# Attention's row maxima taken per 512-query chunk and strewn over two heads, in a hybrid decoder block on one Trainium2 core

## The chip, the core and the metric

The kernel runs on one core of one Trainium2 chip. Its engines are TensorE (PE, matrix products into the accumulation banks, PSUM), VectorE (DVE), ScalarE (ACT), GpSimd (POOL) and SyncE (SP), which here only issues DMAs. Each engine runs its own instructions in order; they wait for one another through semaphores. The metric is the device time of one execution in microseconds (us).

## The reference, cut to what matters

```python
q = (rmsnorm(c_q, g_cq) @ w_uq).reshape(B, S, MLA_HEADS, 96)      # 8 heads, S = 2048
...
for i in range(S // Q_BLOCK):                                     # 128 queries at a time
    s = (jnp.einsum("bqhd,bkhd->bhqk", q_nope[:, q0:q1], k_nope[:, :q1])
         + jnp.einsum("bqhr,bkr->bhqk", q_rope[:, q0:q1], k_rope[:, :q1])) * scale
    p = jax.nn.softmax(jnp.where(causal, s, -jnp.inf), axis=-1)
    outs.append(jnp.einsum("bhqk,bkhd->bqhd", p, v[:, :q1]))
```

This is causal attention over 2048 positions with 8 heads of 96 query and key dimensions and 64 value dimensions. Ahead of it stands one input projection, behind it a gated mixer, a cross-attention into 256 memory tokens and a mixture of 64 experts. All of it is float32, which the kernel makes of fp32r products: each operand x is split into a rounded high part xh and a low part xl = x - xh, and a product is the sum of three.

## The kernel before, in words

The program is a row of blocks: `front` (projections, in 512-token chunks), `attention`, `mix`, cross-attention, routing, experts, combine. Engines meet at a barrier between blocks. The change is in `attention`, with a little in the tail of `front`.

**Units.** Scores are made transposed (keys on partitions, 512 queries in the columns), so that the exponentials can be used as operands at once. A head has 40 units `cols[u] = (c, j)`: query chunk c (0 to 3) against key tile j (0 to 4c+3). The last four units of each chunk lie on the diagonal and have 512, 384, 256 and 128 columns. For unit u PE makes `scores` (three products, L791, L792, L794, and a bf16 mask product L796 on the diagonal) into the ring of four banks `psS`; ACT takes two exponentials of it (`pf` L909, `ph` L910, the second rounded); DVE (odd u, L983) or POOL (even u, L1027) subtracts them to `pl`; PE makes three `products` with the values (L810 to L812). In its loop PE stands at unit u, makes the scores of unit u+3 and the products of unit u-2, so the scores of a head's units 0 to 2 are made at units 37 to 39 of the head before.

**Maxima.** Softmax needs each row's maximum before its first exponential. It is subtracted inside the score product: rows 96 and 97 of `qh` hold minus the maximum (its high and low part) and those of `kh` hold ones. To find it, PE makes plain high-part scores with queries on partitions, in 40 steps `(i, c)` (query tile i, key chunk c, L828, with a mask L830 on the diagonal) into two banks `psA`, and DVE reduces each to `nm` (L944). A last, 41st step turns the 2048 minima: DVE folds `nm` to `mm` (L947), PE transposes it (L821), DVE splits it to `mh` and `ml` (L951, L953), SP sends both to rows 96 and 97 (L716, L717), and the first score product of the head waits for that (`m_in`). The steps of head h+1 are made inside units 11 to 34 of head h, some 1.7 a unit (`a_at`). Head 0's stand by themselves ahead of the units, and the first sixteen alternate with `memory_values`, products for the later cross-attention; before them stand four `memory_keys` (L835).

**Row splits.** A head's q, k and v come by five DMAs (`load`, L707 to L711) to `qraw`, `kraw`, `vraw`. ACT makes the high parts in nine pieces (512 columns of q four times, of k four times, then v; L886, L882) at units 2 to 10, POOL the low parts at units 4, 7, ..., 28 (L1012, L1014); for head 0 DVE makes half of them (L971). SP loads head h+2 once head h+1's splits are done.

Of the kernel before, what the change touches and what calls it, by code (L numbers as in the profile page):

```python
# [16 lines left out]
P = 128  # L17
# [4 lines left out]
CH = 512  # L22
# [77 lines left out]
def front(nc, cst, vec, x, g_mix, w_slabs, pos, w_uq, w_uk, w_uv, gates_d, conv_d, qn_d, qr_d, kn_d, kr_d, v_d,  # L100
          mem, g_mem, w_kv, hh0, hl0, wk_mem, wv_mem, memT, kv_in):
# [9 lines left out]
    with ExitStack() as ctx:  # L111
# [35 lines left out]
        acc = [s_.ps(f"acc{i}", [P, CH]) for i in range(2)]  # L147
# [114 lines left out]
        def _(pe):  # L262
# [71 lines left out]
            for q in range(NC_):  # L334
                for n in range(N):
# [12 lines left out]
                    slab(q, n)  # L348

# [291 lines left out]
def attention(nc, cst, masks, qn_d, qr_d, kn_d, kr_d, v_d, o_d, l_d, wk_mem, wv_mem, memT, kmT, vm, kv_in, km_d, vm_d,  # L641
              w_a, w_b, wb_raw, wa_raw, ar, lr, aT, mixer):
# [7 lines left out]
    rows = [(i, c) for i in range(NT) for c in range(i // 4 + 1)]  # L650
    cols = [(c, j) for c in range(NC_) for j in range(4 * c + 4)]
    NU, NA = len(cols), len(rows) + 1
    RING, AHEAD, PIECES = 4, 3, 2 * NC_ + 1
    PR, LAG = 8, 2
    LO_AT = {4 + 3 * n: n for n in range(PIECES)}
    OUT_AT = {8: 0, 16: 1, 28: 2}
    A0, A1 = 11, 35
    a_at = {}
    for v in range(NA):
        a_at.setdefault(A0 + v * (A1 - A0) // NA, []).append(v)  # L660
    KA, VA = QKD + 2, VD + 2
    with ExitStack() as ctx:
# [16 lines left out]
        mh = s_.sb("mh", [NT, P], F32R)  # L679
        ml = s_.sb("ml", [NT, P], F32R)  # L680
# [3 lines left out]
        psS = [s_.ps(f"psS{i}", [P, CH]) for i in range(RING)]  # L684
# [20 lines left out]
        def _(sp):  # L705
# [30 lines left out]
            load(1)  # L736
            sp.wait_ge(kv_act, 2)
# [30 lines left out]
            for e in range(2):  # L768
                sp.dma_start(lr[e * VD:(e + 1) * VD, :, :], l_d[e:H:2, 0:CM].unsqueeze(0).broadcast_to([VD, H // 2, CM])).then_inc(mixer["ar_in"], 16)
            for c in range(1, NC_):  # L770
                store(H - 1, c)
# [5 lines left out]
        def _(pe):  # L777
            def scores(h, s, u, wait_max):
# [35 lines left out]
            def maxima(h, s, v):  # L814

                b = (s * NA + v) % 2

                pe.wait_ge(a_max, NA * h + v + 1)
                if v == NA - 1:
                    pe.wait_ge(mmin, h + 1)  # L820
                    nc.tensor.transpose(psA[b][0:NT, 0:P], mm_[:], ident).then_inc(a_mm, 1)  # L821
                    return
                i, c = rows[v]
                if v == 0:
                    pe.wait_ge(split_a, PIECES * h + PIECES)
# [19 lines left out]
            for h in range(XH):  # L845
                memory_keys(h)
            pe.wait_ge(set_, 9)
            for v in range(NA):
                maxima(0, 0, v)
                if v < 2 * KD:  # L850
                    memory_values(v // KD, v % KD)
            pe.wait_ge(kv_act, 2)
            pe.wait_ge(kv_dve, 4)
            for u in range(AHEAD):
                scores(0, 0, u, u == 0)

            def head(h, s, more, prev):
                for u in range(NU):
                    if u + AHEAD < NU:
                        scores(h, s, u + AHEAD, False)  # L860
                    elif more:
                        scores(h + 1, 1 - s, u + AHEAD - NU, u + AHEAD == NU)
                    if more:
                        for v in a_at.get(u, []):
# [11 lines left out]
        def _(act):  # L876
            def split(h, s, n):
# [6 lines left out]
                t = slice(n % NC_ * CH, (n % NC_ + 1) * CH)  # L884
                d, r = ((qh, qraw), (kh, kraw))[n // NC_]
# [6 lines left out]
            for b in range(2):  # L892
                act.wait_ge(kv_mm, XH + b + 1)
# [8 lines left out]
            def head(h, s, more, prev):  # L902
                for u in range(NU):
# [11 lines left out]
                    if more and 2 <= u < 2 + PIECES:  # L915
                        if u == 2:

                            act.wait_ge(pv, NU * h + PR)
                        split(h + 1, 1 - s, u - 2)
# [8 lines left out]
        def _(dve):  # L928
# [9 lines left out]
            def top(h, s, v):  # L938
                b = (s * NA + v) % 2
                if v < NA - 1:  # L940
                    i, c = rows[v]
                    w = min(CH, (i + 1) * P - c * CH)
                    dve.wait_ge(a_mm, NA * h + v + 1)
                    V.tensor_reduce(nm[:, i, c:c + 1], psA[b][:, 0:w], AX, ALU.max, negate=True).then_inc(a_max, 1)  # L944
                    return
                dve.wait_ge(a_max, NA * h + v + 2)
                V.tensor_reduce(mm_[:].unsqueeze(2), nm[:], AX, ALU.min).then_inc(mmin, 1)  # L947
                dve.wait_ge(a_mm, NA * h + v + 1)

                dve.wait_ge(m_in, 32 * h + 16)  # L950
                V.tensor_copy(mh[:], psA[b][0:NT, 0:P]).then_inc(mhd, 1)  # L951
                dve.wait_ge(mhd, h + 1)
# [1891 lines left out]
```

## Time and profile before

| | |
|---|---|
| median of 3 runs | 2920.02 us (2916.92 to 2920.36) |
| profiled execution, its time and its span | 2914.94 us, 2913.1 us |
| busy in the span: PE, DVE, ACT, POOL | 92%, 57%, 48%, 23% |
| attention block | 856 to 1423 us of the span |
| mean granted TensorE clock | 0.964 of full speed |

PE's busy time counts pipelined matmuls with modelled ends, so 92% does not say that PE runs at its peak. In the attention block PE is near full in most stretches; what matters is where it isn't, and what ended those waits.

### The profile page before, as it was taken

Reading aid. Unit: us, or ns where it says so; the run is one execution under the profiler, and the core shown is the slowest. Engines: PE = TensorE matmul, PEld = TensorE weight load, DVE = VectorE, ACT = ScalarE, POOL = GpSimd, SP = SyncE. Lnnn points to the kernel's source line nnn. Section 1 sums busy time; section 2 is a strip of 40 time slices with the busy share of each in tenths; the row PEclk is TensorE's granted clock in tenths of the full one; section 3 lists DMA queues with packets and bytes.
Section 4 is the critical chain, followed back from the end, with each engine's and each line's share of the span. In section 5 each row is a group of like instructions: output and inputs, shape, how many; then the busy total and the mean of one; then the engine's idle time right before and its main releaser. Section 6 shows DMA issues by size and latency. Waiting matters only on the chain. (4 is left out here: it accounts for less than half of the span.)

```text
span 2913.1 us, 37842 instructions
## 1 busy us (share of the span) xinstructions
PE 2670.8 (92%) x12830; PEld 2083.5 (72%) x12830; DVE 1669.3 (57%) x2262; ACT 1387.2 (48%) x2316; POOL 665.4 (23%) x708
## 2 busy tenths in 40 slices
PE   6999999999998999999799999899967999999980
PEld 5777787787775666666689898677656777777760
DVE  3623624524426666655554453465566888888858
ACT  4334334324323666667611112543416777777853
POOL 0000000000003555555322220000003444444420
PEclk9999999999998999999899999999978999999995
DMA  4253353354442112212345344232267999999978
GB/s 167 83 189 130 109 171 115 124 171 169 131 134 48 37 39 55 47 37 75 108 131 150 112 134 160 84 109 102 77 255 267 370 373 374 374 383 387 374 279 353
DMA packets 168851, 508.67 MB, mean 175 GB/s; under 512 B 40448, under 2 KB 69760, under 8 KB 140576
## 3 DMA queue, kind: packets, MB, share of 16 engines
q1 hardware_dynamic: 150016, 472.56, 47.4%
q0 software_dynamic: 18720, 34.64, 3.2%
q8 instruction: 64, 1.05, 0.1%
q14 instruction: 51, 0.42, 0.0%
HBM read 432.21 MB, written 108.33 MB: 186 GB/s over the span
## 5 line engine op out<-in xcount | busy, mean ns | idle before, releaser
L487 DVE TENSOR_TENSOR fr_wl<-fr_raw,fr_wh 128x1024 fp32r<-128x1024 f32 x128 | 156.8, 1225 | 470.5 <-ACT fr_wh L358 470.2
L358 ACT CAST fr_wh<-fr_raw 128x1024 fp32r<-128x1024 f32 x128 | 134.0, 1047 | 493.0 <-PE fr_acc L282 493.0
L2547 DVE TENSOR_TENSOR ex_gl<-ba_raw,ex_gh 128x2048 fp32r<-128x2048 f32 x128 | 293.2, 2292 | 101.8 <-ACT ex_gh L2460 101.8
L2460 ACT CAST ex_gh<-ba_raw 128x2048 fp32r<-128x2048 f32 x128 | 245.2, 1917 | 39.5 <-PEq L2055 39.5
L909 ACT ACTIVATE at_pf<-at_psS 128x512 f32<-128x512 f32 (+1 forms) x320 | 178.3, 558 | 167.1 <-PE at_psS L794 84.2
L1027 POOL TENSOR_TENSOR at_pl<-at_pf,at_ph 128x512 fp32r<-128x512 f32 (+1 forms) x160 | 195.4, 1221 | 258.7 <-ACT at_ph L910 258.2
L983 DVE TENSOR_TENSOR at_pl<-at_pf,at_ph 128x512 fp32r<-128x512 f32 (+2 forms) x160 | 145.7, 914 | 139.7 <-ACT at_ph L910 136.5
L944 DVE TENSOR_REDUCE at_nm<-at_psA 128x1 f32<-128x512 f32 (+2 forms) x320 | 183.0, 605 | 63.2 <-PE at_psA L828 43.1
L2397 PE MATMUL ex_psG<-ex_gh,ex_xh 128*128 128x512 f32 x512 | 200.7, 392 | 6.7 <-DVE ex_xl L2552 5.3
L2398 PE MATMUL ex_psG<-ex_gl,ex_xh 128*128 128x512 f32 x512 | 200.3, 391 | 0.0
L2399 PE MATMUL ex_psG<-ex_gh,ex_xl 128*128 128x512 f32 x512 | 200.1, 391 | 0.0
L1003 POOL CAST at_vh<-all_cst 128x32 fp32r<-128x32 f32 x2 | 0.5, 226 | 855.6 <-POOLq L111 855.6
L910 ACT ACTIVATE at_ph<-at_psS 128x512 fp32r<-128x512 f32 (+1 forms) x320 | 177.4, 554 | 0.0
L1239 PE MATMUL mx_psO<-mx_wo_hi,mx_mT 128*128 128x512 f32 x512 | 158.1, 390 | 2.1 <-DVE ea_wo_lo L1372 2.1
L1283 ACT CAST mx_mT<-mx_m 128x256 fp32r<-128x256 f32 x64 | 26.0, 406 | 240.1 <-DVE mx_m L1424 240.1
L282 PE MATMUL fr_acc<-fr_hh,fr_wh 128*128 128x512 f32 x512 | 137.2, 411 | 2.9 <-DVE fr_wl L487 2.9
L282 PE MATMUL fr_acc<-ea_hh,fr_wh 128*128 128x512 f32 x512 | 137.8, 412 | 2.0 <-DVE ea_hl L505 2.0
L828 PE MATMUL at_psA<-at_kh,at_qh 96*128 96x512 f32 (+2 forms) x320 | 118.6, 427 | 19.6 <-DVE at_nm L944 17.6
L791 PE MATMUL at_psS<-at_qh,at_kh 98*128 98x512 f32 (+1 forms) x320 | 122.6, 383 | 9.8 <-DMA at_qh<-at_ml 7.8
L282 PE MATMUL fr_acc<-ea_hh,fr_wl 128*128 128x512 f32 x512 | 126.9, 390 | 0.0
L282 PE MATMUL fr_acc<-fr_hh,fr_wl 128*128 128x512 f32 x512 | 126.8, 390 | 0.0
L282 PE MATMUL fr_acc<-ea_hl,fr_wh 128*128 128x512 f32 x512 | 126.6, 389 | 0.0
(367 smaller groups left out, 6469.7 us busy)
## 6 DMA issues: line engine op xcount, KB each, us to landing
ba_raw<-in_w_exp SPq DMA_DIRECT2D x192, 1024.0 KB, 19.0
fr_raw<-in_w_slabs SPq DMA_DIRECT2D x128, 512.0 KB, 3.8
gates_d<-fr_gst SPq DMA_DIRECT2D x64, 256.0 KB, 4.3
mx_gt<-gates_d SPq DMA_DIRECT2D x64, 256.0 KB, 5.3
cb_ys<-y_d SPq DMA_DIRECT2D x16, 1024.0 KB, 10.9
mx_xr<-in_x SPq DMA_DIRECT2D x8, 1024.0 KB, 7.1
x_d<-mx_xo SPq DMA_DIRECT2D x8, 1024.0 KB, 5.0
xa_xe<-x_d SPq DMA_DIRECT2D x16, 512.0 KB, 5.5
```

The lines of the kernel that those rows point to most:

```text
L282: mm = nc.tensor.matmul(acc[i % 2][:], w[:, i % 2, k, :], h[q % 2][:, k, :], start=(j == 0 and k == 0), stop=(j == 2 and k == KD - 1))
L487: V.tensor_tensor(wl[:, i % 2], raw[:, i % 2], wh[:, i % 2], ALU.subtract).then_inc(w_lo, 1)
L909: nc.scalar.activation(pf[:, u % PR, off:CH], psS[u % RING][:, off:CH], ACT.Exp)
L910: nc.scalar.activation(ph[:, u % PR, off:CH], psS[u % RING][:, off:CH], ACT.Exp).then_inc(hi, 1)
L944: V.tensor_reduce(nm[:, i, c:c + 1], psA[b][:, 0:w], AX, ALU.max, negate=True).then_inc(a_max, 1)
L1027: G_.tensor_tensor(pl[:, r, off:CH], pf[:, r, off:CH], ph[:, r, off:CH], ALU.subtract).then_inc(lo[0], 1)
L1239: mm = nc.tensor.matmul(psO[n][:], mT[:, x_, k, q * P:(q + 1) * P], wop[y_][:, k, hf * CH:(hf + 1) * CH], start=(k == 0 and i == 0), stop= ...
L2397: nc.tensor.matmul(psG[s][:], xh[:, s, f, :], gh[:, s, i, k, :], start=(f == 0), stop=False)
L2398: nc.tensor.matmul(psG[s][:], xh[:, s, f, :], gl[:, s, i, k, :], start=False, stop=False)
L2399: mm = nc.tensor.matmul(psG[s][:], xl[:, s, f, :], gh[:, s, i, k, :], start=False, stop=(f == KD - 1))
L2460: nc.scalar.copy(gh[:, s, i], raw[:, r, i, :].rearrange("p (k n) -> p k n", k=KD // 2)).then_inc(w_hi, 1)
L2547: V.tensor_tensor(gl[:, s, i], raw[:, r, i, :].rearrange("p (k n) -> p k n", k=KD // 2), gh[:, s, i], ALU.subtract).then_inc(w_lo, 1)
```

## The change: what it does

1. The maxima become a stream of 44 `steps`: 40 as before, and a turn for each 512-query chunk, two steps behind the chunk's last maximum. A turn handles four query tiles: `mh` and `ml` are now 4x128, and SP sends a chunk's 512 maxima at a time. The scores of a chunk wait for their own chunk's maxima only.
2. The stream of head h+1 is spread evenly: steps 0 to 26 over units 16 to 39 of head h (`early`), steps 27 to 43 over units 0 to 15 of head h+1 itself (`late`).
3. Head 0 has only its first 16 steps (`PRE`, chunks 0 and 1 with their turns) ahead of the units; the other 28 lie in its own units 0 to 16, and head 1's 27 early steps in its units 17 to 39.
4. ACT's row splits stand at units 3, 5, ..., 19 in the order q0, k0, q1, k1, ...; a maximum waits only for the pieces it reads. In head 0 DVE makes the low parts of k (`key_low`) between its maxima.
5. `memory_keys` of head 0 is made by PE in the tail of `front`, into a bank `bank0` that `front`, `attention` and `mix` now share; three remain in `attention`.
6. SP issues the chunks' maxima between its stores and loads, in the order given below.

The diff, cut to its core (the rest hands `bank0` through):

```diff
+            pe.wait_ge(evac, N * NC_ - 1)
+            for k in range(KD):
+                nc.tensor.matmul(bank0[:, 0:MEM], wk_mem[:, k, 0:XD], memT[:, k, :], start=(k == 0), stop=(k == KD - 1))
...
-    A0, A1 = 11, 35
-    a_at = {}
-    for v in range(NA):
-        a_at.setdefault(A0 + v * (A1 - A0) // NA, []).append(v)
+    steps = []
+    for c in range(NC_):
+        part = [(i, k) for i in range(4 * c, 4 * c + 4) for k in range(c + 1)]
+        steps += part if c == 0 else part[0:2] + [("turn", c - 1)] + part[2:]
+    steps.append(("turn", NC_ - 1))
...
+    PRE, EARLY, TURN2 = 2 * KD, 16, steps.index(("turn", 2))
...
+    BEFORE = sum(EARLY + v * NU // NE < NU for v in range(NE))
+    early, late = spread(range(BEFORE), EARLY, NU), spread(range(BEFORE, NE), 0, EARLY)
+    first_early = spread(range(BEFORE), 17, NU)
+    first_late = {**spread(range(PRE, TURN2 + 1), 0, 7), **spread(range(TURN2 + 1, NE), 7, 17)}
...
             after_split(0)
             load(1)
+            maxima(0, 0, 0)
+            maxima(0, 0, 1)
...
-            maxima(0, 0)
-
-            def head(h, s, more, more2, prev):
+
+            def head(h, s, more2, prev):
+                maxima(h, s, 2)
                 if prev:
                     store(h - 1, 3)
-                for c in range(3):
-                    store(h, c)
+                store(h, 0)
+                maxima(h, s, 3)
+                store(h, 1)
+                maxima(h + 1, 1 - s, 0)
+                store(h, 2)
                 if more2:
                     after_split(h + 1)
                     load(h + 2)
-                if more:
-                    maxima(h + 1, 1 - s)
+                maxima(h + 1, 1 - s, 1)
...
-                if wait_max:
-
-                    pe.wait_ge(m_in, 32 * h + 48)
+                if j == 0:
+
+                    pe.wait_ge(m_in, 32 * NC_ * h + 32 * c + 48)
...
-            for h in range(XH):
+            for h in range(1, XH):
                 memory_keys(h)
             pe.wait_ge(set_, 9)
-            for v in range(NA):
+            for v in range(PRE):
                 maxima(0, 0, v)
-                if v < 2 * KD:
-                    memory_values(v // KD, v % KD)
+                memory_values(v // KD, v % KD)
...
+                    for v in (late if prev else first_late).get(u, []):
+                        maxima(h, s, v)
                     if more:
-                        for v in a_at.get(u, []):
+                        for v in (early if prev else first_early).get(u, []):
                             maxima(h + 1, 1 - s, v)
...
-                    if more and 2 <= u < 2 + PIECES:
-                        if u == 2:
+                    if more and u in HI_AT:
+                        if HI_AT[u] == 0:
...
+            for v in range(PRE):
+                top(0, v)
+                if v % 3 == 0 and v > 0 and v // 3 <= NC_:
+                    key_low(v // 3 - 1)
```

**PE, where head 0's units begin.** Before, the last rows ahead of the first score product (L791) are 25 maxima that stand alone and the turn (L821):

```order
L828 MATMUL at_psA<-at_kh,at_qh 128x512 [waits at_a_max] x4
L830 MATMUL at_psA<-at_neg,at_idb 128x128
L821 MATMUL at_psA<-all_cst,at_mm 16x128 [waits at_mmin,at_a_max]
L791 MATMUL at_psS<-at_qh,at_kh 128x512 [waits at_split_p,at_m_in,at_hi,at_kv_dve,at_kv_act]
L792 MATMUL at_psS<-at_ql,at_kh 128x512
```

Of the changed kernel (L858 are the maxima, L851 a turn, L869 `memory_values`, L821 the first score product, `ea_bank` is `bank0`):

```order
L858 MATMUL at_psA<-at_kh,at_qh 128x512 [waits at_a_max]
L869 MATMUL at_psO<-ea_wv,ea_memT 128x512
L851 MATMUL at_psA<-all_cst,at_mm 4x128 [waits at_mmin,at_a_max]
L869 MATMUL at_psO<-ea_wv,ea_memT 128x512
L821 MATMUL ea_bank<-at_qh,at_kh 128x512 [waits at_split_p,at_m_in,at_hi,at_kv_dve,at_kv_act]
L822 MATMUL ea_bank<-at_ql,at_kh 128x512
```

The 25 steps that stood alone are gone from here; the turn of chunk 1 and a product of `memory_values` are the last things ahead of the scores.

**SP, from the second load of rows to the first store.** Before, behind the loads of head 1 (L707 to L711):

```order
L711 DMA at_vraw<-v_d 128x16x64
L739 DMA km_d<-ea_kmT 128x1024 [waits at_kv_dve,at_kv_act]
L740 DMA vm_d<-ea_vm 128x1024
L716 DMA at_qh<-at_mh 1x16x128 [waits at_mld]
L717 DMA at_qh<-at_ml 1x16x128
L722 DMA o_d<-at_ost 64x512 [waits at_o_out]
```

Now (L733 the last load of head 1, L739 and L740 the maxima of one chunk, L745 a store):

```order
L733 DMA at_vraw<-v_d 128x16x64
L739 DMA at_qh<-at_mh 1x4x128 [waits at_mld]
L740 DMA at_qh<-at_ml 1x4x128
L739 DMA at_qh<-at_mh 1x4x128 [waits at_mld]
L740 DMA at_qh<-at_ml 1x4x128
L764 DMA km_d<-ea_kmT 128x1024 [waits at_kv_dve,at_kv_act]
L765 DMA vm_d<-ea_vm 128x1024
L739 DMA at_qh<-at_mh 1x4x128 [waits at_mld]
L740 DMA at_qh<-at_ml 1x4x128
L745 DMA o_d<-at_ost 64x512 [waits at_o_out]
```

Chunk 0's maxima stand directly behind the five loads of head 1 and no longer behind 41 steps of maxima.

**PE, inside a unit.** Before, a unit in the dense stretch has two maxima between its scores and its products:

```order
L791 MATMUL at_psS<-at_qh,at_kh 128x512 [waits at_hi]
L792 MATMUL at_psS<-at_ql,at_kh 128x512
L794 MATMUL at_psS<-at_qh,at_kl 128x512
L828 MATMUL at_psA<-at_kh,at_qh 128x512 [waits at_a_max] x2
L810 MATMUL at_psO<-at_ph,at_vh 66x384 [waits at_lo_odd]
```

Now most have one:

```order
L821 MATMUL at_psS<-at_qh,at_kh 128x512 [waits at_hi]
L822 MATMUL at_psS<-at_ql,at_kh 128x512
L824 MATMUL at_psS<-at_qh,at_kl 128x512
L858 MATMUL at_psA<-at_kh,at_qh 128x512 [waits at_a_max]
L840 MATMUL at_psO<-at_ph,at_vh 66x256 [waits at_lo_even]
```

The dense stretch of 24 units became an even stream over 40.

## Rows read from the trace of the kernel before

**Rows 1.** Stretches (--windows): us, busy and count of each engine, PEclk, DMA share, GB/s.

```profile
895.00:917.00 22.00, 14.83 (x30) 7.11 (x31) 14.72 (x27) 1.04 (x1) 0.00 (x0) 0.55 0.12 48
917.00:981.00 64.00, 62.67 (x304) 44.31 (x304) 41.07 (x63) 43.40 (x93) 36.30 (x29) 0.94 0.20 40
1111.00:1176.00 65.00, 62.10 (x318) 43.15 (x316) 41.23 (x63) 44.35 (x95) 36.52 (x29) 1.00 0.20 41
```

**Rows 2.** Timeline of PE from the block's start: start, us, engine, line, tiles, [idle before].

```profile
856.13 15.74 PE L835 MATMUL at_psS<-ea_memT,ea_wk 128*128 128x256 f32 x64 [3.94 <-PEq L111]
...
873.66 0.30 PE L828 MATMUL at_psA<-at_kh,at_qh 96*128 96x128 f32 x1 [1.78 <-ACT at_vh L882]
...
878.23 0.45 PE L828 MATMUL at_psA<-at_kh,at_qh 96*128 96x384 f32 x1 [2.18 <-DVE at_nm L944]
...
893.55 0.91 PE L828 MATMUL at_psA<-at_kh,at_qh 96*128 96x512 f32 x2
...
916.68 0.77 PE L791 MATMUL at_psS<-at_qh,at_kh 98*128 98x512 f32 x1 [3.40 <-DMA at_qh<-at_ml]
```

**Rows 3.** Timeline of ACT, DVE and SP in the same stretch.

```profile
868.30 2.18 ACT L886 CAST at_qh<-at_qraw 96x512 fp32r<-96x512 f32 x4 [15.38 <-DMA at_vraw<-v_d]
...
872.42 1.75 DVE L971 TENSOR_TENSOR at_kl<-at_kraw,at_kh 96x512 fp32r<-96x512 f32 x1
...
874.43 3.54 DVE L971 TENSOR_TENSOR at_kl<-at_kraw,at_kh 96x512 fp32r<-96x512 f32 x1
...
878.06 0.48 SPq L707 DMA_DIRECT2D at_qraw<-qn_d  x1
...
880.35 0.50 SPq L711 DMA_DIRECT2D at_vraw<-v_d  x1
...
914.65 0.59 SPq L717 DMA_DIRECT2D at_qh<-at_ml  x1
```

**Rows 4.** DMA issues by tile: count, KB each, median us from issue to landing.

```profile
at_qraw<-qn_d SPq DMA_DIRECT2D x8, 512.0 KB, 4.8
...
at_vraw<-v_d SPq DMA_DIRECT2D x8, 512.0 KB, 9.4
```

**Rows 5.** Timeline of PE: first score product of heads 1 and 7, head 7's end.

```profile
979.80 0.50 PE L791 MATMUL at_psS<-at_qh,at_kh 98*128 98x512 f32 x1 [0.53 <-DMA at_qh<-at_ml]
...
1367.03 0.50 PE L791 MATMUL at_psS<-at_qh,at_kh 98*128 98x512 f32 x1 [0.46 <-DMA at_qh<-at_ml]
...
1419.17 0.22 PE L812 MATMUL at_psO<-at_ph,at_vl 128*66 128x128 f32 x1
```

**Rows 6.** Timeline of PE: starts around maxima steps in head 3.

```profile
1135.92 0.28 PE L828 MATMUL at_psA<-at_kh,at_qh 96*128 96x256 f32 x1
1136.04 0.23 PE L830 MATMUL at_psA<-at_neg,at_idb 128*128 128x128 bf16 x1
1136.08 0.48 PE L828 MATMUL at_psA<-at_kh,at_qh 96*128 96x512 f32 x1
```

**Rows 7.** Waits of PE in 917 to 1390: us in total, times, longest.

```profile
PE at_psA L828 <- DVE at_nm L944: 12.5, 13, 1.4
PE at_psS L791 <- DMA at_qh<-at_ml: 7.8, 8, 3.4
```

**Rows 8.** Timeline of PE, DVE and POOL in head 3, and of DVE in head 7.

```profile
1134.19 0.50 PE L828 MATMUL at_psA<-at_kh,at_qh 96*128 96x512 f32 x1 [1.39 <-DVE at_nm L944]
...
1131.21 2.32 DVE L983 TENSOR_TENSOR at_pl<-at_pf,at_ph 128x512 fp32r<-128x512 f32 x1
...
1131.70 2.96 POOL L1027 TENSOR_TENSOR at_pl<-at_pf,at_ph 128x512 fp32r<-128x512 f32 x2
...
1391.55 0.69 DVE L983 TENSOR_TENSOR at_pl<-at_pf,at_ph 128x512 fp32r<-128x512 f32 x1 [1.60 <-ACT at_ph L910]
```

**Rows 9.** Timeline of ACT in head 0, one unit with a row split.

```profile
926.66 0.61 ACT L886 CAST at_kh<-at_kraw 96x512 fp32r<-96x512 f32 x1
...
928.13 0.63 ACT L886 CAST at_kh<-at_kraw 96x512 fp32r<-96x512 f32 x1
```

More of the change, by code:

```diff
@@ L146, in front @@
         kb = s_.sb("kb", [ROPE, CH])
-        acc = [s_.ps(f"acc{i}", [P, CH]) for i in range(2)]
+        acc = [bank0, s_.ps("acc1", [P, CH])]
         tp = [s_.ps(f"tp{i}", [P, 4, P]) for i in range(2)]
@@ L683, in attention @@
         negT = s_.sb("negT", [P, P], BF16)
-        psS = [s_.ps(f"psS{i}", [P, CH]) for i in range(RING)]
+        psS = [bank0] + [s_.ps(f"psS{i}", [P, CH]) for i in range(1, RING)]
         psA = [s_.ps(f"psA{i}", [P, CH]) for i in range(2)]
@@ L777, in _, with scores @@
         def _(pe):
-            def scores(h, s, u, wait_max):
+            def scores(h, s, u):
                 c, j = cols[u]
@@ L814, in maxima @@
             def maxima(h, s, v):
[L816 to L821, printed above, removed]
+                b, (i, c) = v % 2, steps[v]
+                pe.wait_ge(a_max, NE * h + v + 1)
+                if i == "turn":
+                    pe.wait_ge(mmin, NC_ * h + c + 1)
+                    nc.tensor.transpose(psA[b][0:4, 0:P], mm_[:, 4 * c:4 * c + 4], ident).then_inc(a_mm, 1)
                     return
-                i, c = rows[v]
-                if v == 0:
-                    pe.wait_ge(split_a, PIECES * h + PIECES)
+                if i % 4 == 0 and c == 0:
+                    pe.wait_ge(split_a, PIECES * h + i // 2 + 2)
                 w = min(CH, (i + 1) * P - c * CH)
@@ L945, in top @@
                     return
[L946 to L952, printed above, removed]
-                V.tensor_tensor(ml[:], psA[b][0:NT, 0:P], mh[:], ALU.subtract).then_inc(a_max, 1)
-                dve.wait_ge(a_max, NA * h + v + 3)
+                dve.wait_ge(m_in, 32 * NC_ * h + 32 * c + 16)
@@ L955, in top @@
+                V.tensor_copy(mh[:], psA[b][0:4, 0:P]).then_inc(mhd, 1)
+                dve.wait_ge(mhd, NC_ * h + c + 1)
+                V.tensor_tensor(ml[:], psA[b][0:4, 0:P], mh[:], ALU.subtract).then_inc(a_max, 1)
+                dve.wait_ge(a_max, NE * h + v + 3)
                 dve.sem_inc(mld, 1)
             def memory_keys(h):
-                dve.wait_ge(kv_mm, h + 1)
+                if h > 0:
+                    dve.wait_ge(kv_mm, h)
                 V.tensor_copy(kmT[:, h, :], psS[h][:, 0:MEM]).then_inc(kv_dve, 1)
-            for h in range(XH - 1):
-                memory_keys(h)
@@ L975, in head @@
+            for h in range(XH):
+                memory_keys(h)
+            for v in range(PRE):
+                top(0, v)
+                if v % 3 == 0 and v > 0 and v // 3 <= NC_:
+                    key_low(v // 3 - 1)
             def head(h, s, more, prev):
@@ L983, in head @@
                         V.tensor_tensor(pl[:, r, off:CH], pf[:, r, off:CH], ph[:, r, off:CH], ALU.subtract).then_inc(lo[1], 1)
+                    for v in (late if prev else first_late).get(u, []):
+                        top(h, v)
                     if more:
-                        for v in a_at.get(u, []):
-                            top(h + 1, 1 - s, v)
+                        for v in (early if prev else first_early).get(u, []):
+                            top(h + 1, v)
                     if not more and u in (24, 26, 28, 30):
@@ L1054, in mix @@
         st, eps = s_.sb("st", [P, 4, 3]), s_.sb("eps", [P, 1])
-        psAB = [s_.ps(f"psAB{i}", [P, CH]) for i in range(4)]
+        psAB = [bank0] + [s_.ps(f"psAB{i}", [P, CH]) for i in range(1, 4)]
         psO = [s_.ps(f"psO{i}", [P, CH]) for i in range(2 * NQ)]
```

96 lines of the change are left out of this document (53 added, 43 removed).

## The prediction

> **What bounds the kernel now.** I read the stretches first, then PE's timeline at the start of attention, then its waits, because the change touches only `attention` (and 4 us in the tail of `front`). The attention block has two parts. From 856 to 916.7 nothing of the 320 units runs: PE makes the memory keys, then head 0's maxima; in the 22 us from 895 to 917 it is busy for 14.8 at a granted clock of 0.55, so mostly at the lower of its two levels, 1.2 GHz [rows 1], and the first score product starts at 916.68, released by the DMA of the maxima [rows 2]. That is exposed time: each microsecond by which 916.68 comes earlier is won in full, since everything behind it hangs on PE. From there on PE paces the heads: 62.1 busy of 65 us at full clock, against 41 of DVE, 44 of ACT, 37 of POOL [rows 1]. So the heads get faster only by what PE waits, and I have to size that.
>
> Head 7 has no maxima and no splits inside it. It runs from 1367.03 to 1419.39 = 52.4 us [rows 5]; in this lie the last five product groups of head 6 (512, 512, 384, 256, 128 columns, three products each, at 0.12 us per 256 columns by the spacing in [rows 6], together 2.5). So 40 units alone are 49.9 us of PE. A head's maxima are 28 products of 512 columns, four each of 384, 256 and 128, and 16 masks of 0.04 [rows 6]: 28 x 0.24 + 1.4 + 0.6 = 8.8. An ideal head is 58.7. Heads 1 to 6 take (1367.03 - 979.80) / 6 = 64.5 [rows 5]. So 5.8 us per head is waiting: of it 12.5 / 7 = 1.8 for DVE's maxima and (7.8 - 3.4) / 7 = 0.6 at the head's border for the DMA [rows 7]; the remaining 3.4 are gaps too short for that view, most of them where ACT's splits stand in every unit and a unit takes it 1.47 [rows 9] against 1.1 to 1.4 for PE's six products.
>
> **The change, part by part.**
>
> *The start.* (a) Memory keys: PE idled 3.94 at the border and then took 15.74 for four heads' keys [rows 2]. One head's (3.9) moves into that idle time. It buys nothing directly: the next thing is bound by head 0's rows, which land at 868.3, where ACT's four q casts begin (2.18 for four, 0.54 each [rows 3]). Should it hold the border up, it costs at most a few tenths, which I leave out. (b) The first maximum waited for all nine pieces and began at 873.66 [rows 2]. Now it waits for two, 868.3 + 2 x 0.54 = 869.4. (c) The 14 steps from 878.23 to 893.55 took 1.09 each with their `memory_values` [rows 2]; 16 of them bring PE to 886.9, and I add 1 us of waiting since DVE puts four `key_low` of 1.75 [rows 3] between them: 888. Before, 25 more steps stood behind this, up to 912. They are gone from here. (d) What the first score needs is chunk 0's maxima in `qh`. Their turn is step 6, at about 877, but in SP's order they stand behind `load(1)`, and that behind the last split. The last `key_low` follows step 12: 869.4 + 12 x 1.09 + about 1 for the waits, 0.7 for the maximum, 1.75 for itself, thus 887. SP needs 2.3 us from its first to its last load (878.06 to 880.35 [rows 3]), so the v load is issued at 889.3 and lands 9.4 later, against 4.8 for the q load that is issued first with the same 512 KB or so [rows 4]: later ones land later, a queue served in order. The small transfer stands behind it: 898.7 and half a microsecond, 899.2. Then the first score starts at **899.2 instead of 916.68: 17.5 us less**. Chunk 1's turn on DVE waits until `mh` is free, that is till 899.2, then 0.7 for the turn, 1.2 for the issues and 1.8 for a landing with an empty queue (914.65 to 916.68 less the issue [rows 2, 3]): 903. Its scores come after four others at half clock, 3.6 plus maxima, at about 904. Nothing is lost.
>
> Bounds: were the queue not in order, 890.5 + 2 = 892.9, a gain of 23.8. Were two `key_low` as slow as the pair of 3.54 that met POOL's splits [rows 3], 4 us later, a gain of 13.5.
>
> *Head 0* (63.1 from 916.68 to 979.80 [rows 2, 5]). It now holds 26 maxima and 2 turns of its own and 25 and 2 of head 1, where it held 40 and 1: 11 x 0.24 + 3 x 0.1 = 2.9 more. A turn is a 128-column transpose; I take 0.1 (between 0.04 and 0.24). PE idles for ten microseconds ahead of the first score as before, so I expect the same half clock for the first units; six maxima that now lie in it cost double, 1.2. Its first 17 units carry 28 steps, 1.65 per unit, as dense as before, so the waits for DVE stay there (2.8), while the second half gives back 3. Together **+3.9**.
>
> *Heads 1 to 6.* 44 steps in 40 units, never more than two in one, mostly one. A wait for a maximum comes up when DVE is late by two steps, since `psA` has two banks. At two steps per unit that is one unit, at one step two units, 3.2 us. The longest wait, 1.39, was made by a subtraction L983 of 2.32 us that ran beside POOL's work, where undisturbed it is 0.69 [rows 8]; 2.32 plus a maximum of 0.69 is 3.0, which now fits. ACT's splits in every second unit make a pair 1.47 + 0.95 = 2.4 against PE's 2.8 to 3.3: the gaps there go. The wait at the border goes too: chunk 0's turn is at unit 21 and its scores at 37. I leave 0.5 of waiting, and 3 turns more: 58.7 + 0.3 + 0.5 = 59.5. Six heads: **-30**. The bounds are 58.9 (-34) and 62.5, where 3 of the 5 us stay (-12).
>
> Three places where a late transfer could take the gain's place. Chunk 1's maxima of head h+1 (turn at unit 29) stand behind `load(h+2)`, issued near unit 28 and landing 12 us later by the same rows, at unit 36; their scores are made at unit 1 of the next head, five units (8 us) later. Chunk 2's turn, unit 0, has 3 us of transfer against 9 units. Chunk 3's, unit 15, has 6 units; in the last head SP must first get past the store of chunk 0 (unit 8), the wait for its landing and three loads, for which it has seven units, 10 us.
>
> *Head 7* gets 12 x 0.24 + 0.4 + 0.2 of masks + 2 turns = 3.6 that lay in head 6, and some waiting: **+4.0**. DVE's divisions there start at unit 24, behind the last turn.
>
> Sum: -17.5 + 3.9 - 30 + 4.0 = -39.6. The profiled execution took 2914.94, so 2875.3; the median of the runs shown is 5.1 above that execution, their lowest 2.0. I forecast **2878**.
>
> **Two rules of the Trainium skill.** The row shows L983 at 2.32 beside POOL and 0.69 alone [rows 8]. The Trainium skill ("SBUF — State Buffer", section "SBUF: two separate sides") says that VectorE and GpSimd hold a shared port pair in turns for a whole instruction, also for a VectorE operation with two SBUF inputs; by that rule the trace agrees, and since the change removes none of POOL's work the blocking stays and speaks against the full gain. The Trainium skill ("DMA: Bandwidth & Descriptors", section "Queues, rings and completion order") says that each DMA engine consumes a ring in order, but that a small DMA which uses few rings may complete ahead of a large earlier one; landing times of [rows 4] agree with the first half, no row shows the second.
>
> **Rivals.**
> A, *the blocking by POOL stays dear* (0.16). POOL's nine splits and twenty subtractions per head are where they were, and DVE gets small turn operations besides (four turns instead of one). For it: 1.39 at POOL's split of unit 13 [rows 8]. Against: DVE is busy 41 of 59.5 us. If 3 us of waiting stay per head: +18, 2896. The first rule above names this mechanism.
> B, *chunk 0's maxima overtake the load* (0.10). It would give 892.9: 6.3 less, 2872. This is what the second rule's second half would do. Against: landings of [rows 4] grow with the order.
> C, *chunk 1's maxima land late* (0.04), the one that ends slower. Their transfer needs to land 8 us later than reckoned before PE waits at all; each further microsecond then costs one in each of seven heads. All the gain is spent at 39.6 / 7 = 5.7 beyond, that is 13.7 us later than reckoned; at 15 it would cost 7 x 7 = 49, and the time be 2927. In the rows a load takes 9.4 to land, not 25.
> D, *the start gains nothing* (0.04): if the first score stayed at 916, with 2.9 and 1.2 still paid, 2895.
>
> **How the numbers follow.** My forecast has 0.66. Its own range is 2866 to 2889 (start 13.5 to 19, heads -34 to -22). To hold 8 in 10 the range takes in B, and A and D up to 2896: **2863 to 2898**. No change and measurement uncertainty are told apart at 0.2%, 5.8 us. Faster: all but C and the tail, 0.94; same 0.03; slower 0.03.
>
> **What would show it.** First score at 899 (b to d right), with PE idle for ten microseconds ahead of it and the wait put down to the DMA of `mh` or `ml`; 893 says B. Distance between heads' first scores 59.5; 61 and more, with waits for `at_nm` above 1 us near units 13 and 28, says A. No wait for `m_in` inside heads; one at unit 1 says C. Head 0 at 67. I would be wrong mostly if DVE's order (each odd unit's subtraction waits for ACT ahead of that unit's maxima) makes a wait where PE now needs every single maximum soon after it is made.

## The result, and the profile after

The changed kernel takes **2876.65 us** (median of 4, 2871.8 to 2879.95) against 2918.53 (2916.92 to 2920.36, 4) of the kernel before on the same chip: ratio 0.9857, 95% interval 0.9844 to 0.9869. On a second chip it took 2875.14 us, ratio 0.9859 (0.9845 to 0.9873). The prediction was 2878, and its steps can be followed in the profiled execution, whose span is 2870.0 us against 2913.1. Of `no_idle`, below, one execution of six (3092.5 us at a mean granted clock of 0.834) was in a second, slower state and is left out.

The stretches answer to [rows 1] (us, busy and count of PE, PEld, DVE, ACT, POOL, then PEclk, DMA share, GB/s). The first line is the stretch ahead of head 0, the second the one around its first score product, the last two are heads 0 and 1:

```profile
887.00:897.00 10.00, 0.42 (x1) 0.00 (x0) 0.00 (x0) 1.87 (x2) 0.00 (x0) 0.65 1.00 196
...
895.00:917.00 22.00, 19.59 (x77) 14.36 (x78) 10.30 (x22) 12.30 (x27) 8.34 (x7) 0.65 0.19 59
...
897.00:963.00 66.00, 65.59 (x312) 47.37 (x313) 42.94 (x80) 43.96 (x92) 36.56 (x29) 0.90 0.23 55
963.00:1023.00 60.00, 60.00 (x318) 43.58 (x317) 41.59 (x73) 43.86 (x93) 37.54 (x29) 1.00 0.22 46
```

A head takes 60 us in which PE is listed as busy all the time; before it was 65, with 2.9 not busy. What remains idle is the stretch ahead of head 0: one PE instruction from 887 to 897. PE's timeline there answers to [rows 2], and its last three lines to [rows 5]:

```profile
850.64 3.61 PE L355 MATMUL ea_bank<-ea_memT,ea_wk 128*128 128x256 f32 x16
854.74 10.60 PE L865 MATMUL at_psS<-ea_memT,ea_wk 128*128 128x256 f32 x48 [0.48 <-PEq L111]
867.93 0.30 PE L858 MATMUL at_psA<-at_kh,at_qh 96*128 96x128 f32 x1 [2.60 <-ACT at_kh L917]
...
870.01 1.31 PE L858 MATMUL at_psA<-at_kh,at_qh 96*128 96x384 f32 x1
...
886.39 1.02 PE L869 MATMUL at_psO<-ea_wv,ea_memT 128*128 128x512 f32 x2
897.39 0.77 PE L821 MATMUL ea_bank<-at_qh,at_kh 98*128 98x512 f32 x1 [9.97 <-issue]
...
963.02 0.40 PE L821 MATMUL ea_bank<-at_qh,at_kh 98*128 98x512 f32 x1
...
1322.43 0.40 PE L821 MATMUL ea_bank<-at_qh,at_kh 98*128 98x512 f32 x1
...
1379.31 0.22 PE L842 MATMUL at_psO<-at_ph,at_vl 128*66 128x128 f32 x1
```

Its waits in 897 to 1380 are a single line, where [rows 7] had over 20 us (the one left is the wait at 897.39, which the profile puts down to "issue"):

```profile
PE ea_bank L821 <- issue: 10.0, 1, 10.0
```

What that wait was for is shown by SP and DVE (answering to [rows 3]). DVE's second turn writes `mh` as soon as chunk 0's two transfers have been read out of it, 0.1 us ahead of the first score:

```profile
884.96 0.48 SPq L729 DMA_DIRECT2D at_qraw<-qn_d  x1
...
887.25 0.50 SPq L733 DMA_DIRECT2D at_vraw<-v_d  x1
887.79 6.51 SPq L739 DMA_DIRECT2D at_qh<-at_mh  x1
894.35 0.62 SPq L740 DMA_DIRECT2D at_qh<-at_ml  x1
897.96 0.57 SPq L739 DMA_DIRECT2D at_qh<-at_mh  x1
...
884.20 0.68 DVE L995 TENSOR_TENSOR at_kl<-at_kraw,at_kh 96x512 fp32r<-96x512 f32 x1
...
897.29 0.28 DVE L981 CAST at_mh<-at_psA 4x128 fp32r<-4x128 f32 x1 [10.97 <-DMA at_qh<-at_ml]
```

The attention block began at 856.0 before and at 854.6 now (DVE's first instruction in it). With each time taken from there:

| us | before | after | change | predicted |
|---|---|---|---|---|
| first score product | 60.7 | 42.8 | -17.9 | -17.5 |
| head 0 | 63.1 | 65.6 | +2.5 | +3.9 |
| heads 1 to 6, together | 387.2 | 359.4 | -27.8 | -30 |
| head 7 | 52.4 | 57.1 | +4.7 | +4.0 |
| end of PE's work in attention | 563.4 | 524.9 | **-38.5** | -39.6 |

Outside it the block began 1.4 earlier, and 3.2 came off after it, spread over later stages, whose work did not change; that makes the 43.1 of the spans. Neither is the change's doing as far as these runs show: in the twelve traces of this document the block begins between 850.8 and 857.6 (in the second trace of the changed kernel at 857.6), and what follows it takes 1490 to 1498. For experiments I give "the end", this last line, beside the time, because it isn't touched by such drift. It has a scatter of its own: the six traces whose start is as in the changed kernel, or differs from it by the memory keys alone, have the first score 41.7 to 43.3 us after the block's start, so the end is to be read to about 1 us.

### The profile page after: what moved, and what is told of

Read it like the earlier page. It is cut to its first block and busy times, and to the rows that moved or that the text cites. A ratio compares the mean times of both kernels' runs of the same rounds, so it can differ in the third digit from the quotient of the medians.

```text
span 2870.0 us, 38196 instructions
## 1 busy us (share of the span) xinstructions
PE 2651.3 (92%) x12854; PEld 2085.2 (73%) x12854; DVE 1668.3 (58%) x2334; ACT 1390.1 (48%) x2316; POOL 671.8 (23%) x708
## 5 line engine op out<-in xcount | busy, mean ns | idle before, releaser
L940 ACT ACTIVATE at_pf<-at_psS 128x512 f32<-128x512 f32 (+3 forms) x240 | 125.2, 522 | 80.7 <-PE at_psS L824 41.9
L1012 DVE TENSOR_TENSOR at_pl<-at_pf,at_ph 128x512 fp32r<-128x512 f32 (+2 forms) x160 | 132.1, 825 | 13.9 <-ACT at_ph L941 11.8
L858 PE MATMUL at_psA<-at_kh,at_qh 96*128 96x512 f32 (+2 forms) x320 | 128.5, 416 | 2.6 <-ACT at_kh L917 2.6
L941 ACT ACTIVATE at_ph<-at_psS 128x512 fp32r<-128x512 f32 (+3 forms) x240 | 123.9, 517 | 0.0
L2447 PE MATMUL ex_psY<-ba_raw,ex_hT 128*128 128x512 f32 x256 | 120.6, 593 | 2.8 <-ACT ex_hT L2510 2.2
L840 PE MATMUL at_psO<-at_ph,at_vh 128*66 128x512 f32 (+1 forms) x320 | 121.7, 380 | 0.0
L2428 PEld LDWEIGHTS ex_psG<-ex_gh,ex_xh 128*128 128x128 f32 x512 | 96.5, 189 | 28.0 <-DVE ex_xl L2583 5.7
L842 PE MATMUL at_psO<-at_ph,at_vl 128*66 128x512 f32 (+1 forms) x320 | 115.3, 361 | 0.0
L841 PE MATMUL at_psO<-at_pl,at_vh 128*66 128x512 f32 (+1 forms) x320 | 115.1, 360 | 0.0
L1270 PEld LDWEIGHTS mx_psO<-mx_wo_hi,mx_mT 128*128 128x128 f32 x512 | 96.2, 189 | 22.0 <-DVE ea_wo_lo L1403 2.3
```

Source lines behind the costliest of these rows:

```text
L858: mm = nc.tensor.matmul(psA[b][:, 0:w], qh[0:QKD, s, i * P:(i + 1) * P], kh[0:QKD, s, c * CH:c * CH + w], start=True, stop=not diag)
L1012: V.tensor_tensor(pl[:, r, off:CH], pf[:, r, off:CH], ph[:, r, off:CH], ALU.subtract).then_inc(lo[1], 1)
L1270: mm = nc.tensor.matmul(psO[n][:], mT[:, x_, k, q * P:(q + 1) * P], wop[y_][:, k, hf * CH:(hf + 1) * CH], start=(k == 0 and i == 0), stop= ...
L2428: nc.tensor.matmul(psG[s][:], xh[:, s, f, :], gh[:, s, i, k, :], start=(f == 0), stop=False)
```

## Experiments

**How much of the start is the load in front of the maxima? Two edits and both together.** In `m0_first` SP sends chunk 0's maxima ahead of `load(1)`; in `v_behind` the v load leaves `load` and gets a semaphore of its own, so that it can be issued behind the maxima.

```diff
+            maxima(0, 0, 0)
             after_split(0)
             load(1)
-            maxima(0, 0, 0)
             maxima(0, 0, 1)
```

```diff
-                sp.dma_start(vraw[:], v_d[...]).then_inc(raw_in, 16)
+            def load_v(h):
+                sp.dma_start(vraw[:], v_d[...]).then_inc(v_in, 16)
...
             load(0)
+            load_v(0)
...
             maxima(0, 0, 1)
+            load_v(1)
...
                 maxima(h + 1, 1 - s, 1)
+                if more2:
+                    load_v(h + 2)
...
                 if n == 0:
-                    act.wait_ge(raw_in, 80 * h + 80)
+                    act.wait_ge(raw_in, 64 * h + 64)
                 if n == PIECES - 1:
+                    act.wait_ge(v_in, 16 * h + 16)
```

> The changed kernel, with SP sending chunk 0's maxima of head 0 ahead of the load of head 1's rows (and ahead of its wait for the splits). If the first score waits only because that transfer stands behind the load, chunk 0 lands near 880 and the first score starts when PE's prelude ends, near 888 instead of 897.4; chunk 1's maxima still stand behind the load, so PE then waits until about 897 at its fifth unit, which started at 902.7: 5 to 6 us less in all. Rival: the first score waits for something else (the copies of the memory values, the row splits): first score unchanged, 0 us.

> The changed kernel, with each head's v load (2048 pieces of 256 bytes) issued behind the maxima instead of ahead of them, on a semaphore of its own. Theory 1: what holds SP for 6.5 us at the issue of mh is the many small pieces of v in the queue. Then the issue takes 0.6 us, the maxima land behind the bytes of q and k alone, the first score starts near 894 (3 to 4 us earlier), and the heads keep 59.9. Theory 2: any full queue holds it, q and k too: the issue still takes several us, the first score stays at 897, 0 us.

> Both of the two edits before. First score near 888, chunk 1's maxima behind q and k only, landing near 894, where PE waits some 2 us at its fifth unit (about 894 against 902.7), and PE has no idle stretch of 10 us any more, so the half clock of the first units (about 4 us of loss) may shrink: 9 to 13 us less in all. If theory 2 of the v load holds: as m0_first, 5 to 6 us less.

Measured (the ratio is against the kernel before):

| | us | ratio, 95% | first score | head 0 | end |
|---|---|---|---|---|---|
| after | 2876.65 | 0.9857, 0.9844 to 0.9869 | 42.8 | 65.6 | 524.9 |
| m0_first | 2872.42 | 0.9837, 0.982 to 0.9853 | 33.8 | 68.55 | 518.9 |
| v_behind | 2868.38 | 0.9834, 0.9813 to 0.9854 | 37.8 | 64.9 | 519.1 |
| both | 2870.23 | 0.9829, 0.9812 to 0.9845 | 31.4 | 66.6 | 514.6 |

The ends order what the times, some 5 us wide each, can't. SP's timeline of `v_behind`, the loads of q and k and then the maxima:

```profile
880.87 0.58 SPq L733 DMA_DIRECT2D at_kraw<-kr_d  x1
881.50 0.76 SPq L742 DMA_DIRECT2D at_qh<-at_mh  x1
882.31 0.61 SPq L743 DMA_DIRECT2D at_qh<-at_ml  x1
...
890.36 0.45 SPq L736 DMA_DIRECT2D at_vraw<-v_d  x1
890.92 1.08 SPq L769 DMA_DIRECT2D km_d<-ea_kmT  x1
```

Without the v load ahead of it the issue of `mh` takes 0.76 instead of 6.51. Yet the first score (888.56 in that trace) still stands 5.6 us behind the end of the second issue, where the kernel before, with nothing else in the queue, needed about 1.4 (914.65 + 0.59 to 916.68 [rows 2, 3]): the maxima wait for the q and k loads. So the queue is served in order here, as predicted. The gain of 5.0 has two parts, though: ACT's casts for head 0 no longer wait for head 0's own v either (the first maximum comes 12.1 after the block's start instead of 13.3, the last product of the prelude, PE's work ahead of head 0's units, at 29.8 instead of 31.8), which is 2.0, and 3.0 are left for the v load in the queue. Of the 11.4 us that the first score gains in `both`, 6.4 more are then the other four loads; PE's prelude ends there too, so a larger gain could not show. In `m0_first` the hold moves to chunk 1 (SP L739 at 890.11 takes 6.05) and PE waits for it four scores later:

```profile
890.28 0.50 PE L821 MATMUL ea_bank<-at_qh,at_kh 98*128 98x512 f32 x1 [0.68 <-ACT ea_vm L925]
...
899.16 0.79 PE L821 MATMUL ea_bank<-at_qh,at_kh 98*128 98x512 f32 x1 [5.83 <-DMA at_qh<-at_ml]
```

Of 9.0 us gained at the first score 3.0 are given back in head 0. The ends are 6.0, 5.9 and 10.3 us earlier, as expected for `m0_first` (5 to 6) and `both` (9 to 13); for `v_behind` 3 to 4 were expected, and the 2.0 of the prelude came on top.

**All of the loads behind both chunks: `no_idle`.** `v_behind`, with this order on SP, and the splits of head 1 moved from unit 3 to 7 (ACT) and from 4 to 8 (POOL) in head 0, so that they wait for no load.

```diff
-            after_split(0)
-            load(1)
             maxima(0, 0, 0)
             maxima(0, 0, 1)
+            after_split(0)
+            load(1)
+            load_v(1)
```

> The changed kernel, with v behind on a semaphore of its own, both chunks' maxima of head 0 sent ahead of all loads of head 1, and, since those then land some 8 us later, ACT's and POOL's row splits inside head 0 moved from units 3 to 19 and 4 to 28 to units 7 to 23 and 8 to 32. If the two waits at the start are the transfers' and the half clock of head 0's first units comes from the idle time ahead of them, PE now goes from the prelude into the units with under 1 us of waiting, the clock stays at its upper level, chunk 1's scores start 3.5 us after the first score instead of 5.3 to 8.9, and head 0 takes 60 to 61 instead of 65 to 68: PE's end, counted from the block's start, 10 us less than with the two edits before, 20 less than the changed kernel's. Rival: the units' own pattern keeps the clock low there: head 0 stays at 64 or more, and only the 3.5 us of wait are won.

Measured: 2859.93 us (the changed kernel on the same chip: 2875.14), ratio 0.9807 (0.9794 to 0.982). First score 31.4, chunk 1's scores 2.9 after it, head 0 61.4, the end 509.5: 15.4 less than the changed kernel, 5.1 less than `both` with the same first score. The expectation had 20 and 10. The difference is in head 0, and the stretches show why (`both`, then `no_idle`):

```profile
895.00:905.00 10.00, 10.00 (x42) 6.85 (x41) 6.10 (x13) 6.22 (x13) 5.62 (x5) 0.75 0.13 51
```

```profile
895.00:905.00 10.00, 9.87 (x55) 7.16 (x54) 8.79 (x16) 7.32 (x17) 6.20 (x5) 1.00 0.76 191
```

Both have PE busy, but `both` had waited 3.5 us for chunk 1's maxima just before, ran at a granted clock of 0.75 there, and did 42 matmuls where `no_idle` did 55 at 1.00. In the microsecond slices of the trace `both` is at 0.50 to 0.60 from 893 to 900, and `no_idle` is at 1.00 in every one from 885 to 925. So idle time at the start was paid twice, once as idle and once as half clock in head 0's first units. The splits of head 1 moved in the same edit, and what they did to head 0 wasn't tried by itself: the wait (3.5) and half of the 7 us at the lower clock would make 7.0, and head 0 is 5.2 shorter. This version beats both kernels.

**The memory keys: `keys_back`** puts head 0's `memory_keys` back into attention and leaves all else.

> The changed kernel, with the memory keys of head 0 made in the attention block again. PE idles 2.6 us there between its keys and the first maximum; a fourth head of keys takes 3.6, so the first maximum comes 1.0 later and the total is 1 us more. Rival: the 3.6 us moved into the tail of the block before were a gain of their own: 3.6 us more.

Measured: 2878.8 us, ratio 0.9864 (0.9847 to 0.988). The first maximum is 2.2 us later from the block's start, the first score 42.9 instead of 42.8, the end 524.9, the same. The 2.2 us did not reach the end. One reason is PE's clock. The changed kernel idles 2.60 us ahead of its first maximum, and its third (870.01, in PE's timeline above) takes 1.31; `keys_back` has no such gap:

```profile
860.61 10.52 PE L859 MATMUL at_psS<-ea_memT,ea_wk 128*128 128x256 f32 x48
870.78 0.41 PE L852 MATMUL at_psA<-at_kh,at_qh 96*128 96x128 f32 x1
...
873.31 0.23 PE L854 MATMUL at_psA<-at_neg,at_idb 128*128 128x128 bf16 x1
873.38 1.08 PE L863 MATMUL at_psO<-ea_wv,ea_memT 128*128 128x512 f32 x2
```

The stretch from 870 to 873 of the changed kernel, then of `keys_back`:

```profile
870.00:873.00 3.00, 3.00 (x7) 1.19 (x5) 0.56 (x1) 1.86 (x3) 3.00 (x3) 0.51 0.00 0
```

```profile
870.00:873.00 3.00, 3.00 (x15) 1.87 (x13) 1.05 (x3) 3.00 (x7) 3.00 (x4) 1.00 0.00 0
```

(`keys_back` has its slow stretch earlier, at 0.50 to 0.70 from 856 to 860, in the keys themselves, behind 3.93 us of idle; that is part of its later first maximum.) SP's first load of head 1 is 0.6 us later there (31.0 against 30.4), and the shorter hold of SP (5.82 instead of 6.51) takes the rest. The 3.6 us of the rival are out; 1.0 us is at the edge of what the end resolves.

**Head 0's maxima ahead of its units again: `start_back`** (`PRE = NE`, `first_late = {}`).

> The changed kernel, with all 44 steps of head 0 ahead of its units. DVE's second turn waits until the first transfer has landed (897) and holds the 28 steps behind it, 0.75 us each: first score near 918, head 0 itself shorter by 28 steps of about 0.25, near 58: 14 us more in all (the heads 1 to 7 as they are). If the start were worth nothing because head 0 pays it back inside: 0 to 3 us more.

Measured: 2886.4 us, ratio 0.9895 (0.9875 to 0.9916). First score 64.4, head 0 56.6, the end +12.8 (14 were expected). Moving 28 steps from ahead of the units into them is worth 21.6 at the first score, and head 0 takes 9.0 of it back. That is a price in this order alone: PE first waits 9.76 us here too, for chunk 0's maxima to leave `mh` (DVE's second turn), and 27 of the 28 steps then run at a granted clock of 0.50.

**Which edit makes the heads shorter? `splits_dense`, `stream_dense`, `both_dense`.** The first puts ACT's splits into units 2 to 10, the second the 44 steps into units 11 to 34 (SP's order follows), the third does both.

```diff
-    HI_AT, LO_AT = ({a + b * n: n for n in range(PIECES)} for a, b in ((3, 2), (4, 3)))
+    HI_AT, LO_AT = ({a + b * n: n for n in range(PIECES)} for a, b in ((2, 1), (4, 3)))
```

```diff
-    early, late = spread(range(BEFORE), EARLY, NU), spread(range(BEFORE, NE), 0, EARLY)
-    first_early = spread(range(BEFORE), 17, NU)
+    early, late = spread(range(NE), 11, 35), {}
+    first_early = spread(range(NE), 17, 39)
```

> The changed kernel, with ACT's nine row splits in units 2 to 10 again instead of every second unit. Theory A: the spacing carries a third of the heads' gain: ACT needs 1.47 us a unit there, DVE's subtractions wait for it and the maxima behind them too, so the heads go from 59.9 to 61 or 62, 8 to 12 us more in all. Theory B: the even stream gives PE 1.5 to 1.65 us of work in these units, enough to cover ACT: heads at 60.2 or less, 0 to 2 us more.

> The changed kernel, with all 44 steps of head h+1 in units 11 to 35 of head h again (in head 0: units 17 to 38), chunk turns kept, row splits in every second unit. Theory A: the even spread carries most of the heads' gain: waits for at_nm come back, 2 to 3 us per head in heads 1 to 6, heads at 62 to 63, and head 0's second half, now with two steps a unit, costs a few us besides; 15 to 20 us more in all. Theory B: the splits and the earlier turns carried it: heads at 60 to 61, at most 6 us more.

> The changed kernel with both the stream packed into units 11 to 35 and the splits in units 2 to 10: what is left of the change in the heads is the turn per chunk. Alone they cost 9.6 and 9.8 us. If they are separate causes: 19 to 20 us more, heads 2 to 6 at 63.4 to 64, within a microsecond of the kernel before (64.4). If one covers the other: 12 to 15 more, heads at 62.5.

Measured: `splits_dense` 2884.92 us, ratio 0.9887 (0.987 to 0.9905), the end +9.7, heads 1 to 6 61.6 on average; `stream_dense` 2889.7, 0.9902 (0.9881 to 0.9923), +9.6, a middle head 61.4, so between its two theories (15 to 20, at most 6); `both_dense` 2909.76, 0.9977 (0.9967 to 0.9987), +29.3, a middle head 64.0. Together they cost 10 us more than the sum of the two, which neither branch of the last expectation had. Of these 10, 7.5 lie in heads 1 to 6, 0.7 in head 0 and 1.8 ahead of the first score, where the three kernels don't differ. To see where in the heads, I took the distances between the first score products of neighbouring units in heads 2 to 5, from the traces, and subtracted PE's own work in each (its products and steps by their columns, at 0.2335 us for 512, the spacing of products that follow without a gap, and 0.04 for a mask). What is left is waiting, in us per head; "units" are the places in PE's loop, where it makes the scores of three units on:

```
units          0-4   5-10  11-13  14-16  17-25  26-28  29-34  35-36  37-39   sum
before         0.2   1.7   0.3    1.9    0.7    1.2    0.5    0.9    0.2     7.5
after          0.3   0.6   0.0    0.2    0.6    0.1    0.2    0.3    0.3     2.7
splits_dense   0.3   0.6   0.0    1.9    0.6    0.1    0.2    0.3    0.3     4.4
stream_dense   0.2   0.3   0.3    0.7    1.0    0.9    0.4    0.2    0.1     4.1
both_dense     0.2   1.8   0.3    1.9    1.0    0.9    0.4    0.2    0.1     6.8
```

- Units 5 to 10: 1.7 are lost only where the splits are dense and the units hold no maxima. A unit of PE's six products is 1.0 to 1.4 us there in `stream_dense`, and 1.49 in `both_dense` and before, which is ACT's unit with a split (1.47, [rows 9]). Either of the change's two measures removes this loss by itself: sparse splits relieve ACT, and an even stream gives PE work that covers them. This is why the two cost more together: 1.0 us a head by the table's sums, 4 of the 10 us in these four heads. Another 3.5 lie in heads 1 and 6, which I did not take apart.
- Units 14 to 16: 1.9 wherever the splits are dense, with the maxima spread or not. In `splits_dense` this is a mean: 2.6 in heads 2 and 4, 1.3 in heads 3 and 5, and why they alternate wasn't looked into. PE's only listed waits between 950 and 1330 are here, two in each head:

```profile
PE at_psA L858 <- DVE at_ml L983: 5.2, 6, 1.5
PE at_psA L851 <- DVE at_mm L977: 2.5, 6, 0.4
```

  and the timeline of POOL, DVE and PE in head 4 shows a subtraction of DVE (L1012) of 2.85 us beside POOL's subtractions and splits; the turn's `mh` and `ml` (L981, L983) stand behind it, and the second maximum behind them:

```profile
1168.35 2.99 POOL L1058 TENSOR_TENSOR at_pl<-at_pf,at_ph 128x512 fp32r<-128x512 f32 x2
...
1171.30 1.29 POOL L1043 TENSOR_TENSOR at_ql<-at_qraw,at_qh 96x512 fp32r<-96x512 f32 x1
...
1171.53 2.85 DVE L1012 TENSOR_TENSOR at_pl<-at_pf,at_ph 128x512 fp32r<-128x512 f32 x1
...
1172.54 1.29 POOL L1058 TENSOR_TENSOR at_pl<-at_pf,at_ph 128x512 fp32r<-128x512 f32 x1
...
1174.61 0.28 DVE L983 TENSOR_TENSOR at_ml<-at_psA,at_mh 4x128 fp32r<-4x128 f32 x1
1174.94 0.38 PE L858 MATMUL at_psA<-at_kh,at_qh 96*128 96x256 f32 x1 [1.50 <-DVE at_ml L983]
```

  At the same turn and head of the changed kernel POOL waits for ACT, and DVE's subtraction is through in 0.89:

```profile
1167.90 1.29 POOL L1058 TENSOR_TENSOR at_pl<-at_pf,at_ph 128x512 fp32r<-128x512 f32 x1 [1.63 <-ACT at_ph L941]
...
1168.85 0.89 DVE L1012 TENSOR_TENSOR at_pl<-at_pf,at_ph 128x512 fp32r<-128x512 f32 x1
1169.16 1.74 POOL L1043 TENSOR_TENSOR at_ql<-at_qraw,at_qh 96x512 fp32r<-96x512 f32 x1
```

  So the loss looks like rival A's mechanism and not like a pace of ACT's. That the loss comes and goes with the splits is measured; that ACT's splits do it by holding POOL back is read from that one wait, and wasn't tried by itself.
- Units 17 to 28 lose 1.3 more where the stream is dense: that is the stream's own part. Waits for `at_nm` came back, as its theory A had it, but only 3.4 us in six heads and not 2 to 3 in each.
- Units 35 and 36, the wait for the DMA of all maxima (0.9), went in every version with turns by chunk.

Head 0 and head 7 belong to the stream as well: in `stream_dense` head 0 takes 70.3 (its own 28 steps and all 44 of head 1), head 7 52.2.

## Why the prediction was right, step by step

**The start, -17.9 against -17.5.** The memory keys "buy nothing": measured 0.0 at the end, to about 1 us. The first maximum came 13.3 after the block's start, reckoned 13.4. The last `key_low` ended at 884.9, reckoned 887: the four took 0.68 each and not 1.75. (The 1.75 was read beside POOL's splits; here the first `key_low` starts at 874.32, when POOL's prelude, up to 874.44, is all but done.) The block began 1.4 earlier too, so the mis-sizing was below 1 us of the sum. Three slips of the working did no harm: the terms given for 887 add up to 885.9, a landing in an empty queue is 1.4 by the rows named and not 1.8, and the bound 892.9 should be 892.5. The v load landed 9.6 after its issue (9.4 reckoned), and the first score followed it by half a microsecond, as reckoned. That SP itself is held for 6.51 us in the issue of `mh` was not foreseen. By the landings it costs nothing at the first score, since the transfer would have landed behind v in any case; no run had the one without the other. Chunk 1 lost nothing: its `mh` was issued at 897.96, its scores began 5.3 us after the first, and no wait stands there.

**Rival B** (chunk 0's maxima overtake the load) is out by `v_behind`: with v gone the maxima still waited for q's and k's loads. And the first score came at 42.8 and not 36.9. The Trainium skill ("DMA: Bandwidth & Descriptors", section "Queues, rings and completion order") leaves room for a small DMA that finishes ahead of a large earlier one; no run here showed it, with 2 KB behind 512 KB. **Rival D** is out by the first score itself, and by `start_back`.

**Head 0, +2.5 against +3.9.** The number was near, but two of its terms were wrong, in opposite directions. "The same half clock for the first units" was not the same. PE's idle time ahead of the first score was 9.97 in one piece, where before it was 3.40 just ahead of it, and the lower clock lasts 13 us into the head instead of 8 (before, then after):

```profile
917.00:925.00 8.00, 8.00 (x26) 5.90 (x26) 1.03 (x2) 6.25 (x15) 3.12 (x3) 0.53 0.01 3
```

```profile
897.00:911.00 14.00, 13.61 (x42) 9.98 (x43) 5.29 (x12) 7.31 (x16) 4.59 (x5) 0.52 0.20 77
```

PE is busy all through both, so I estimate 2.7 us for the 5.3 us more at half clock, where the forecast had 1.2. Against that, the waits of 2.8 that I left in for the dense first half are not in the list of waits. The other parts can't be taken apart.

**Heads 1 to 6, -27.8 against -30.** A head takes 59.9 and not 59.5. The parts of the gain, by the table of waits: the gaps at the splits 1.1 (units 5 to 10), the waits for DVE 1.7 and 1.1 (units 14 to 16 and 26 to 28), the border 0.6. I had put most of 3.4 us of short gaps down to ACT's splits in every unit; this was the mis-sized step, although the sum held. The "ideal head" of 58.7 was mis-sized too: it is built on head 7's 49.9, which holds waits itself. By the columns a head before is 64.5 - 7.5 = 57.0 of work. So 4.8 us of 7.5 went, and 2.7 stay; the forecast had 5.3 of 5.8, and 0.5. Sparse splits do act in units 5 to 10, but in the changed kernel the stream alone covers that (0.6 in `splits_dense` too), and what is left for them to bring is the 1.7 at units 14 to 16.

**Head 7, +4.7 against +4.0**: 1.1 more than the 3.6 of its moved steps, where I had left 0.4 for "some waiting".

**Rival A**: absent from the changed kernel (no wait for DVE in its list), but 1.9 us per head away from it, as `splits_dense` shows. By the Trainium skill ("SBUF — State Buffer", section "SBUF: two separate sides") VectorE and GpSimd take turns at a shared port for a whole instruction; the trace agrees, 2.85 us beside POOL's work and 0.89 at the same place with less overlap. The rule alone does not say when the two collide; by the one wait read above, the price hangs on when ACT releases each. **Rival C**: no wait stands inside the heads.

**The total.** That 2878 met 2876.65 within 1.4 us is in part luck. The drift outside attention, -4.6 in the spans, was not in the sum; attention itself gave 1.1 less than forecast, and the median lies 4.9 above the profiled execution, where I had added 2.7. The three nearly cancel. What the mechanism has to answer for is the -38.5 against -39.6.

## What to carry to other kernels

Spread a stream of small work so that every unit of the bottleneck engine holds some: it covers the helper engines' bursts. Here the dense splits cost nothing in units 5 to 10 under the even stream, nor did the thin units there without dense splits; the two together cost 1.2 more. Count in a transfer's price what stands ahead of it in its queue, and send the small one that somebody waits for first; here that was worth another 10 us, and 15 with the second chunk's maxima ahead of the loads too. Idle time of PE can cost itself and then half clock behind it: removing the last wait of 3.5 us, with head 1's splits moved, made the end 5.1 earlier.

## What the runs showed that was not expected

An issue on SP behind a v load (512 KB in pieces of 256 bytes, with four loads just before it) holds SP for microseconds, whatever is issued: 6.51 for `mh` at the start, and in a middle head of the changed kernel

```profile
1011.73 0.50 SPq L731 DMA_DIRECT2D at_kraw<-kn_d  x1
...
1013.05 0.43 SPq L733 DMA_DIRECT2D at_vraw<-v_d  x1
1013.58 6.48 SPq L739 DMA_DIRECT2D at_qh<-at_mh  x1
1020.11 0.63 SPq L740 DMA_DIRECT2D at_qh<-at_ml  x1
```

where most issues elsewhere in attention take 0.3 to 0.7. In `both` and `no_idle` it hit the transfer of `km_d` instead (4.95 and 6.39); in `v_behind`, with v issued 9 us after the other four, only 1.08. The kernel before issued v in the same way (1031.13), but nothing behind it for 10 us, so its trace could not show it. In 17 places with a hold that I compared (ten at the start of as many traces, seven in a later head) it ended between 0.1 us before and 1.6 us after the time at which the load of `kn_d`, two ahead of v, should have landed (its issue plus the median 7.4). That would fit a queue with limited room, which comes free as earlier loads end, but this is a guess: no run varied the size of the pieces, so the cause stays open. In the middle heads it costs PE nothing: the second issue ends at 1020.74 above, and chunk 1's first score product starts at 1028.71.
